# Gathering tokens for a mixture of experts: one transfer of whole 4 KB rows in place of three transfers of 1 KB quarters

## The chip, the cores and the metric

The kernel runs on 1 core of one Trainium2 chip, as one program written for its five engines by hand: TensorE (PE), VectorE (DVE), ScalarE (ACT), GpSimd (POOL) and SyncE (SP). The metric is the device time in microseconds, from the first to the last instruction with what lies around them; the numbers are medians of several runs.

## The reference

Two transformer blocks follow each other over 512 tokens of 1024 floats. The first has a convolution and FFT mixer, a cross attention over 256 memory rows and a mixture of 32 experts, the second two kinds of attention and a dense feed-forward layer. Only the mixture of experts is touched by the change. Cut to what matters:

```python
logits = hf @ w_router + b_router                 # 512 x 32
top_v, top_i = lax.top_k(logits, 4)               # 4 experts of each token
top_w = softmax(top_v)
# for every expert e, over the tokens that chose it:
gu = h[tok] @ w_gate_up[e] + b_gate_up[e]         # 1024 -> 2048
gate = minimum(gu[:, :1024], 7); up = clip(gu[:, 1024:], -7, 7)
glu = gate * sigmoid(1.702 * gate)
y[tok] += top_w * (((up + 1) * glu) @ w_down[e] + b_down[e])
```

All of it is float32. An expert's weights are 8 MB and 4 MB, so 32 experts read 384 MB from HBM. Each expert gets 64 tokens on average.

## The kernel before

A block of the expert stage is one expert with up to `CAP` = 96 slots for tokens (3 groups of 32, `GROUPS` and `QUAD`); a slot without a token is out of bounds for the transfers and is skipped. With these inputs there are 32 blocks. The stage is a loop on each engine.

SP loads the weights in chunks of 1 MB into a ring of 12 slots (`ring_a`, `ring_b`, L557 to L600): 8 chunks of `w_gate_up` and 4 of `w_down` for each block. A load waits on `m_used`, which TensorE raises as it is through with the slot's last chunk.

TensorE (`moe_tensor`, L1940) works on 32 columns of the array at a time: four products side by side, for four quarters j of the output columns. So both operands must have the contraction index on the partitions, and the tokens of a group on 32 free places. `gate_up_open` (L1954) multiplies a one-hot `pick` with the biases and then waits for the tokens, `m_x`. `gate_up_chunk` (L1965, the product is L1970) takes `xe` and a chunk. After the 8 chunks of block n+1 come the 4 `down_chunk` (L1977, product L1984) of block n, with `act_t`. In the midst of the gate and up products `slot_sums` (L1944, product L1947) finds which token sits in which slot; it waits for VectorE's `select`.

The tokens lie in HBM as `h_rows`, 2048 rows of 256 floats: row 4*t+j is quarter j of token t. POOL's `gather` (L743) issues one indirect DMA for each of the three groups (L749). Partition 32*j+s of group g receives quarter j of the token in slot 32*g+s, into `xg[:, g, :]`. The row numbers `idx[0]` are made by `indices` (L1547) on VectorE. VectorE then turns all 32x32 blocks of `xg` with one instruction into `xe` (`x_transpose`, L1575, instruction L1579): in each quarter of the partitions a 32x32 block at a time. The same row numbers, one and two blocks later, serve `scatter` (L752, L757), which adds the weighted outputs onto `x_rows` in HBM.

The order of a block on VectorE is written out at L1613 to L1618: `select` (L1526: which slot holds which token), `indices` (it waits for the scatter two blocks back, since it overwrites its row numbers), `swiglu` (L1581: it takes the sums out of PSUM at L1586 and L1587, waits for ACT's Silu, and makes `act_e` at L1590 and L1593), `pick_row` (L1561), `x_transpose`, and `act_transpose` (L1573: it waits until the down products of the last block are done). `link` puts a semaphore behind an instruction for the next one on VectorE that reads it. Before the loop the first two blocks are done by the same functions, with `route_weights` between them.

`hold` is a small POOL instruction in front of each group of indirect DMAs. `m_gathered` counts 16 for each transfer.

Of the kernel before, what the change touches and what calls it, by code (L numbers as in the profile page):

```python
# [22 lines left out]
GROUPS, QUAD = 3, 32  # L23
CAP = GROUPS * QUAD
PASSES = -(-SEQ // CAP)
MAXB = NE * PASSES
QF = D // 4
# [17 lines left out]
C_EXP = C_TOK + T  # L45
C_OWN = C_EXP + NE
C_QUAD = C_OWN + P
C_EYE = C_QUAD + 1
C_ALL = C_EYE + MAXB + 1

S_CONV, S_GC, S_GF, S_ALL = 0, 12, 16, 20
# [3 lines left out]
def shape_constants():  # L55

    p = np.arange(P)
    c = np.zeros((P, C_ALL), np.float32)
    c[:, C_IDENT:C_IDENT + P] = np.eye(P)
    c[:, C_FLIP:C_FLIP + P] = np.eye(P)[::-1]  # L60
    c[:, C_ONES:C_ONES + P] = 1.0
    c[:, C_STRICT:C_STRICT + P] = p[:, None] < p[None, :]
    c[:, C_NTRI:C_NTRI + P] = -(p[:, None] >= p[None, :]).astype(np.float32)
    c[:, C_NONES:C_NONES + P] = -1.0
    g = np.arange(64)
    w = 2 * np.pi * np.outer(g, g) / 64
    for b in range(2):
        s = slice(64 * b, 64 * b + 64)
        c[s, C_BDC + 64 * b:C_BDC + 64 * b + 64] = np.cos(w) / 8
        c[s, C_BDS + 64 * b:C_BDS + 64 * b + 64] = -np.sin(w) / 8  # L70
    c[:, C_SLOT:C_SLOT + P] = p[None, :]
    n = np.arange(MAXB + 1)
    c[:, C_OWN:C_OWN + P] = np.arange(P)[None, :] % QUAD == p[:, None] % QUAD
    c[:, C_QUAD] = p // QUAD
    c[:, C_TOK:C_TOK + T] = P * np.arange(T)[None, :] + p[:, None] + CAP
    c[:, C_EXP:C_EXP + NE] = np.arange(NE)
    c[:, C_EYE:] = n[None, :] % NE == p[:, None] % NE
    s = np.arange(SEQ)
    w = 2 * np.pi * (np.outer(s, s) % SEQ) / SEQ
    dft = np.stack([np.cos(w), np.sin(w)]).astype(np.float32) * np.float32(SEQ ** -0.5)  # L80
    rel = np.arange(SPAN) - (SEQ - 1)
    dist = np.abs(rel)
    far = np.maximum(dist, 1).astype(np.float32)
    large = 8 + (np.log(far / np.float32(8)) / np.float32(math.log(16)) * np.float32(8)).astype(np.int32)
    bucket = (rel > 0) * 16 + np.where(dist < 8, dist, np.minimum(large, 15))
    onehot = (np.arange(32)[:, None] == bucket[None, :]).astype(np.float32)
    return c, dft.astype(np.float32), onehot
# [26 lines left out]
def program(nc, A, out):  # L114
    ctx = ExitStack()
    with ctx:
# [3 lines left out]
        def at(name, offset, shape, dt=F32):  # L120
            plan[name] = (offset, int(np.prod(shape[1:])) * 4)
            return nc.alloc_sbuf_tensor_at(name, shape, dt, offset=base + offset)

        def sem(n):
            return ctx.enter_context(nc.semaphore(n))
# [24 lines left out]
        K = lambda k: AR + int(k * KB)  # L150
# [12 lines left out]
        probs = at("probs", K(0), [P, 2, T, MEM])  # L163
        probsT = at("probsT", K(48), [P, 2, MT, SEQ])

        xg = at("xg", K(0), [P, GROUPS, QF])
        xe = at("xe", K(4), [P, GROUPS, QF])
        glu = at("glu", K(12), [P, GROUPS, QF])
        up1 = at("up1", K(15), [P, GROUPS, QF])
# [2 lines left out]
        ye = at("ye", K(24), [P, GROUPS, QF])  # L172
        bias_gu = at("bias_gu", K(36), [3 * NE, 2 * D], BF16)
        sel = at("sel", K(40), [P, T, CAP])
        small_i = lambda i: K(41.875) + 32 * i
        slot_s = at("slot_s", small_i(1), [P, 2, GROUPS])
        slot_w = at("slot_w", small_i(9), [P, GROUPS])
        row_f = at("row_f", small_i(10), [P, GROUPS])
        idx = [at(f"idx{i}", small_i(3 + i), [P, GROUPS], I32) for i in range(3)]
# [73 lines left out]
        h_dram = nc.dram_tensor("h_rows", [SEQ * 4, QF], F32, kind="Internal").ap()  # L253
# [4 lines left out]
        cc = lambda c, n=P: const[:, c:c + n]  # L258
# [484 lines left out]
        def gather(pool, n, k):  # L743

            pool.wait_ge(m_idx, n + 1)
            pool.wait_ge(m_x, n)
            hold(pool, k)
            for g in range(GROUPS):
                pool.indirect_dma_start(xg[:, g, :], None, h_dram, bass.IndirectOffsetOnAxis(ap=idx[0][:, g:g + 1].bitcast(U32), axis=0),  # L749
                                        bounds_check=SEQ * 4 - 1, oob_is_err=False).then_inc(m_gathered, 16)  # L750

        def scatter(pool, n, k, rows):  # L752

# [6 lines left out]

        def moe_moves(pool):
            pool.wait_ge(r_table, 1)
            pool.memset(xg[:, :, :], 0.0).then_inc(xg_zero, 1)
            pool.wait_ge(xg_zero, 1)
            pool.wait_ge(m_scat, 16)
            pool.wait_ge(x_set, 16 * T)
            n1 = pool.value_load(n_blk[0:1, 0:1], min_val=NE - 1, max_val=MAXB - 1)
            gather(pool, 0, 0)
            gather(pool, 1, 1)
            with pool.Fori(0, n1) as i:  # L770
                gather(pool, i + 2, i * 2 + 2)
                scatter(pool, i, i * 2 + 3, idx[2])
            scatter(pool, n1, n1 * 2 + 2, idx[1])
# [742 lines left out]
        def moe_vector(dve, link_route):  # L1516
            dve.wait_ge(r_table, 1)
            n1 = dve.value_load(n_blk[0:1, 0:1], min_val=NE - 1, max_val=MAXB - 1)
            steps, base_ = [0], [0]

            def link(i):
                i.then_inc(moe_dve_step, 1)
                steps[0] += 1
                dve.wait_ge(moe_dve_step, base_[0] + steps[0])
# [22 lines left out]
            def indices(n, scattered, gathered, parts=2):  # L1547

                dve.wait_ge(m_pos, n + 1)
                if scattered is not None:  # L1550
                    dve.wait_ge(m_scat, scattered)
                if gathered is not None:
                    dve.wait_ge(m_gathered, gathered)
                dve.tensor_copy(idx[2][:, :], idx[1][:, :])  # L1554
                link(dve.tensor_copy(slot_w[:, :], slot_s[:, 1, :]))
                dve.tensor_copy(idx[1][:, :], idx[0][:, :])
                link(dve.tensor_copy(slot_s[:, 0:parts, :].rearrange("p a g -> p (a g)"), ps[:, 6, 0:parts * GROUPS]))
                link(dve.tensor_scalar(row_f[:, :], slot_s[:, 0, :], 4.0, cc(C_QUAD, 1), ALU.mult, ALU.add))
                dve.tensor_scalar(idx[0][:, :], row_f[:, :], 4.0 * CAP, None, ALU.subtract).then_inc(m_idx, 1)

            def pick_row(n, used):  # L1561

# [5 lines left out]
            flat = lambda b: b[:, :, :].rearrange("p g c -> p (g c)")  # L1568

            def act_transpose(n, used):  # L1570
                dve.wait_ge(m_act, n + 1)
                dve.wait_ge(m_used, used)
                dve.transpose(flat(act_t), flat(act_e)).then_inc(m_at, 1)  # L1573

            def x_transpose(n, used):  # L1575
                dve.wait_ge(m_gathered, n * 48 + 48)
                if used is not None:
                    dve.wait_ge(m_used, used)
                dve.transpose(flat(xe), flat(xg)).then_inc(m_x, 1)  # L1579

            def swiglu(n, used):  # L1581

                dve.wait_ge(m_used, used)
                dve.wait_ge(m_bias_sb, n + 1)
                bias = lambda u: bias_b[:, QF * u:QF * u + QF].unsqueeze(1).to_broadcast([P, GROUPS, QF])
                dve.tensor_tensor(glu[:, :, :], ps[:, 0:GROUPS, 0:QF], bias(0), ALU.add).then_inc(m_sum, 1)  # L1586
                dve.scalar_tensor_tensor(up1[:, :, :], ps[:, 0:GROUPS, QF:2 * QF], 1.0 / ALPHA, bias(1),  # L1587
                                         ALU.mult, ALU.add).then_inc(m_sum, 1)
                dve.wait_ge(m_sum, n * 2 + 2)
                link(dve.tensor_scalar(up1[:, :, :], up1[:, :, :], (1.0 - LIMIT) / ALPHA, (1.0 + LIMIT) / ALPHA, ALU.max, ALU.min))  # L1590
                dve.wait_ge(m_at, n)
                dve.wait_ge(m_glu, n + 1)
                dve.scalar_tensor_tensor(act_e[:, :, :], glu[:, :, :], SILU_TOP, up1[:, :, :], ALU.min, ALU.mult).then_inc(m_act, 1)  # L1593
# [7 lines left out]
            x_transpose(0, None)  # L1601
            route_weights(dve, link_route)
            select(1, 0)
            indices(1, None, 48)
            swiglu(0, 8)
            pick_row(1, 8)
            x_transpose(1, 8)
            act_transpose(0, 8)
            done = steps[0]
            steps[0] = 0  # L1610
            with dve.Fori(0, n1) as i:
                base_[0] = i * 7 + done
                select(i + 2, i + 1)  # L1613
                indices(i + 2, i * 48 + 16, i * 48 + 96)
                swiglu(i + 1, i * 12 + 16)
                pick_row(i + 2, i * 12 + 9)
                x_transpose(i + 2, i * 12 + 16)
                act_transpose(i + 1, i * 12 + 20)  # L1618
            assert steps[0] == 7, steps

        def ffn_vector(dve):
            def gate_up(j):
# [466 lines left out]
```

## Time and profile before

| | us |
|---|---|
| median of 3 runs | 2207.1 (2205.42 to 2207.76) |
| the profiled execution, its own time | 2204.74 |
| its span, first to last instruction | 2202.8 |
| PE busy | 2075.9 (94%) |
| DVE busy | 865.7 (39%) |
| ACT busy | 478.9 (22%) |
| POOL busy | 359.7 (16%) |

The profile describes one execution. The expert stage lies between about 411 and 1462 us of the span, nearly half of it. Its page gives the work of all DMA queues: the hardware queue of SP moved 496.01 MB, the software queue of POOL 24.85 MB, at 237 GB/s over the whole span and 403 to 410 GB/s in most slices of the expert stage. A matmul's time is modelled and pipelined, so a busy TensorE is not one at its peak. In brackets behind a row stands the engine's idle time before the instruction, and who ended it.

### The profile page before, as it was taken

To read this page: it belongs to the slowest core of one execution; us is meant where nothing else is said; L and a number is where in the kernel's file an instruction comes from. 1 tells how busy PE (TensorE), PEld (TensorE's weight loads), DVE (VectorE), ACT (ScalarE), POOL (GpSimd) and SP (SyncE) were. 2 spreads that over 40 slices of the span, in tenths; PEclk is the share of its full clock that TensorE was granted. 3 is DMA by queue.
4 is the path that set the end of the run, shared out by engine and by line. 5 is a ranking of instruction groups with operands and counts; after the bars stand their busy time and mean duration, and the time that the engine had idled before them with its cause. 6 is when DMAs were issued, how large, how long until landed. Compare 5 with 4: busy or idle time off the path is not lost.

```text
span 2202.8 us, 41891 instructions
## 1 busy us (share of the span) xinstructions
PE 2075.9 (94%) x17404; PEld 1255.0 (57%) x17404; DVE 865.7 (39%) x1468; ACT 478.9 (22%) x749; POOL 359.7 (16%) x389
## 2 busy tenths in 40 slices
PE   6999898499999999999999999979998998999998
PEld 5879777234344434433443333337775777888887
DVE  4444434432333233333333333333565433444444
ACT  4242333000000000000000000023445723122221
POOL 1010001112222222222223222231201200000000
PEclk9999999699999999999999999979998999999999
DMA  6325111999999999999999999973111022233230
GB/s 235 116 77 166 58 39 40 354 348 403 405 404 410 405 405 405 410 403 404 403 405 402 404 408 396 399 256 106 58 58 39 1 65 70 76 99 111 77 113 38
DMA packets 157840, 521.53 MB, mean 237 GB/s; under 512 B 16428, under 2 KB 71776, under 8 KB 124928
## 3 DMA queue, kind: packets, MB, share of 16 engines
q1 hardware_dynamic: 137008, 496.01, 57.7%
q0 software_dynamic: 20784, 24.85, 4.7%
q8 instruction: 35, 0.57, 0.1%
q14 instruction: 13, 0.11, 0.0%
HBM read 510.65 MB, written 18.88 MB: 240 GB/s over the span
## 4 chain that ended last, share of the span: by engine, by line
PE 60%; DMA 9%; SPq 4%; DVE 3%; ACT 2%; POOL 1%; issue 1%; ACTq 0%; DVEq 0%; POOLq 0%
PE ps L1970 21%; PE ps L1984 11%; PE ps L390 8%; PE ps L392 8%; PE ps L391 8%; DMA ring_a<-in_w_down 6%; SPq L567 3%; DMA ring_a<-in_w_gate_up 2%; SPq L565 2%; PE ps L1879 1%; PE ps L492 1%; POOL rstd L464 1%; PE ps L1871 1%; PE ps L1889 1%; PE ps L1832 0%
## 5 line engine op out<-in xcount | busy, mean ns | idle before, releaser
L1970 PE MATMUL ps<-ring_a,xe 128*32 128x512 f32 x3912 | 436.0, 596 | 12.2 <-DVE xe L1579 10.6
L1984 PE MATMUL ps<-ring_a,act_t 128*32 128x256 f32 x6000 | 333.5, 379 | 5.5 <-DMA ring_a<-in_w_down 3.8
L1970 PEld LDWEIGHTS ps<-ring_a,xe 128*32 128x32 f32 x3912 | 124.8, 110 | 297.0 <-issue 254.3
L1984 PEld LDWEIGHTS ps<-ring_a,act_t 128*32 128x32 f32 x6000 | 193.6, 110 | 153.0 <-issue 21.5
L1970 PE MATMUL ps<-ring_b,xe 128*32 128x512 f32 x2232 | 251.5, 593 | 0.0
L390 PE MATMUL ps<-xt_hi,hi 128*128 128x512 f32 x576 | 228.8, 397 | 5.6 <-DVE xt_lo L505 4.7
L392 PE MATMUL ps<-xt_hi,lo 128*128 128x512 f32 x576 | 226.4, 393 | 0.0
L391 PE MATMUL ps<-xt_lo,hi 128*128 128x512 f32 x576 | 226.2, 393 | 0.0
L1073 ACT ACTIVATE glu<-glu 128x768 f32<-128x768 f32 x32 | 27.0, 843 | 649.1 <-DVE glu L1586 649.1
L757 POOL DMA_INDIRECT x_rows<-ye,idx x96 | 154.3, 1607 | 37.8 <-issue 37.8
L390 PE MATMUL ps<-hi,xt_hi 128*128 128x512 f32 (+1 forms) x384 | 147.4, 384 | 7.4 <-DVE lo L377 5.2
L1970 PEld LDWEIGHTS ps<-ring_b,xe 128*32 128x32 f32 x2232 | 69.1, 110 | 149.7 <-issue 143.1
L377 DVE TENSOR_TENSOR lo<-raw,hi 128x2048 fp32r<-128x2048 f32 x46 | 106.2, 2314 | 106.1 <-ACT hi L370 103.9
L391 PE MATMUL ps<-lo,xt_hi 128*128 128x512 f32 (+1 forms) x384 | 144.8, 377 | 0.0
L392 PE MATMUL ps<-hi,xt_lo 128*128 128x512 f32 (+1 forms) x384 | 144.8, 377 | 0.0
L1554 DVE COPY idx<-idx 128x3 int32<-128x3 int32 x33 | 5.6, 169 | 338.7 <-DMA x_rows<-ye,idx 332.2
L741 POOL TENSOR_TENSOR held_x<-minus_half 128x1 f32<-128x1 f32 x65 | 12.5, 192 | 713.3 <-ACT ye L1079 368.9
L390 PEld LDWEIGHTS ps<-xt_hi,hi 128*128 128x128 f32 x576 | 109.7, 190 | 29.8 <-DVE xt_lo L505 5.5
L391 PEld LDWEIGHTS ps<-xt_lo,hi 128*128 128x128 f32 x576 | 109.7, 191 | 23.2 <-issue 0.5
L392 PEld LDWEIGHTS ps<-xt_hi,lo 128*128 128x128 f32 x576 | 109.3, 190 | 23.1
L370 ACT ACTIVATE hi<-raw 128x2048 fp32r<-128x2048 f32 x46 | 87.6, 1911 | 103.6 <-PE ps L392 103.6
L749 POOL DMA_INDIRECT xg<-h_rows,idx x99 | 102.7, 1037 | 38.8 <-issue 38.8
(297 smaller groups left out, 2475.4 us busy)
## 6 DMA issues: line engine op xcount, KB each, us to landing
ring_a<-in_w_gate_up SPq DMA_DIRECT2D x163, 1024.0 KB, 20.8
ring_a<-in_w_down SPq DMA_DIRECT2D x125, 1024.0 KB, 23.5
ring_b<-in_w_gate_up SPq DMA_DIRECT2D x93, 1024.0 KB, 19.5
raw<-in_w_in SPq DMA_DIRECT2D x20, 1024.0 KB, 7.7
raw<-in_w_gate SPq DMA_DIRECT2D x11, 1024.0 KB, 5.4
raw<-in_w_up SPq DMA_DIRECT2D x11, 1024.0 KB, 5.4
raw<-in_w_down SPq DMA_DIRECT2D x11, 1024.0 KB, 4.8
raw<-in_w_out SPq DMA_DIRECT2D x8, 1024.0 KB, 5.0
```

The source lines that it names most:

```text
L370: act.activation(hi[:, c % HL, :], raw[:, c % RAW, :], ACT.Copy).then_inc(S.hi_ready, 1)
L377: dve.tensor_tensor(lo[:, c % HL, :], raw[:, c % RAW, :], hi[:, c % HL, :].bitcast(F32), ALU.subtract).then_inc(S.lo_ready, 1)
L390: pe.matmul(dst_, l_hi, r_hi, start=first, stop=False)
L391: pe.matmul(dst_, l_hi, r_lo, start=False, stop=False)
L392: return pe.matmul(dst_, l_lo, r_hi, start=False, stop=last)
L565: sp.dma_start(m_slot(slot), src.squeeze(0) if len(src.shape) == 3 else src).then_inc(m_raw[slot], 16)
L567: sp.dma_start(m_slot(slot).rearrange("p (k n) -> p k n", k=2), src).then_inc(m_raw[slot], 16)
L749: pool.indirect_dma_start(xg[:, g, :], None, h_dram, bass.IndirectOffsetOnAxis(ap=idx[0][:, g:g + 1].bitcast(U32), axis=0), bounds_check=S ...
L757: pool.indirect_dma_start(x_dram, bass.IndirectOffsetOnAxis(ap=rows[:, g:g + 1].bitcast(U32), axis=0), ye[:, g, :], None, bounds_check=SEQ ...
L1073: act.activation(glu[:, :, :], glu[:, :, :], ACT.Silu, scale=ALPHA).then_inc(m_glu, 1)
L1970: last = pe.matmul(ps[QUAD * j:QUAD * j + QUAD, g, :], xe[:, g, QUAD * k:QUAD * k + QUAD], w[:, j, :, :, :], start=k == 0, stop=k == KT - 1)
L1984: last = pe.matmul(y_block(g, j), act_t[:, g, QUAD * (2 * c + h):QUAD * (2 * c + h) + QUAD], w[:, h, QF * j:QF * j + QF], start=c == 0 and ...
```

## The change

The gather becomes one transfer for 96 slots: partition s receives the whole row of 1024 floats of slot s's token. Its row numbers, one for each partition, are made by three more small VectorE instructions: the slot table `slot_s` has, on every partition 32*q+s, the token of slot 32*g+s in column g; the new constant `C_GRP` is one where g equals q, so product and sum pick the token of slot 32*q+s. The table `idx[0]` of the scatter stays as it was.

In `xg` group g now lies in the partitions 32*g to 32*g+31, and quarter q in the columns 256*q to 256*q+255. The transposes therefore read one quarter of the partitions and write another: 12 instructions of 32x256, one for each q and g, in place of one of 128x768. `xe` is the same as before.

`swiglu` is cut in two. `add_bias` (the two additions out of PSUM) stays where it was; the rest comes behind `pick_row` and `x_transpose`.

```diff
-        xg = at("xg", K(0), [P, GROUPS, QF])
+        xg = at("xg", K(0), [P, D])
...
-            for g in range(GROUPS):
-                pool.indirect_dma_start(xg[:, g, :], None, h_dram, bass.IndirectOffsetOnAxis(ap=idx[0][:, g:g + 1].bitcast(U32), axis=0),
-                                        bounds_check=SEQ * 4 - 1, oob_is_err=False).then_inc(m_gathered, 16)
+            pool.indirect_dma_start(xg[0:CAP, :], None, h_dram.rearrange("(s j) c -> s (j c)", j=4),
+                                    bass.IndirectOffsetOnAxis(ap=idx_g[0:CAP, 0:1].bitcast(U32), axis=0),
+                                    bounds_check=SEQ - 1, oob_is_err=False).then_inc(m_gathered, 16)
...
-                dve.tensor_scalar(idx[0][:, :], row_f[:, :], 4.0 * CAP, None, ALU.subtract).then_inc(m_idx, 1)
+                dve.tensor_scalar(idx[0][:, :], row_f[:, :], 4.0 * CAP, None, ALU.subtract)
+                link(dve.tensor_tensor(row_g[:, :], slot_s[:, 0, :], cc(C_GRP, GROUPS), ALU.mult))
+                link(dve.reduce_sum(row_1[:, :], row_g[:, :], AX.X))
+                dve.tensor_scalar(idx_g[:, :], row_1[:, :], float(CAP), None, ALU.subtract).then_inc(m_idx, 1)
...
-                dve.wait_ge(m_gathered, n * 48 + 48)
+                dve.wait_ge(m_gathered, n * 16 + 16)
                 if used is not None:
                     dve.wait_ge(m_used, used)
-                dve.transpose(flat(xe), flat(xg)).then_inc(m_x, 1)
+                for q in range(4):
+                    for g in range(GROUPS):
+                        i = dve.transpose(xe[QUAD * q:QUAD * q + QUAD, g, :], xg[QUAD * g:QUAD * g + QUAD, QF * q:QF * q + QF])
+                i.then_inc(m_x, 1)
...
                 select(i + 2, i + 1)
-                indices(i + 2, i * 48 + 16, i * 48 + 96)
-                swiglu(i + 1, i * 12 + 16)
+                indices(i + 2, i * 48 + 16, i * 16 + 32)
+                add_bias(i + 1, i * 12 + 16)
                 pick_row(i + 2, i * 12 + 9)
                 x_transpose(i + 2, i * 12 + 16)
+                swiglu(i + 1)
                 act_transpose(i + 1, i * 12 + 20)
```

The blocks ahead of the loop are changed in the same way, and the memset of `xg` covers 1024 columns.

## Rows read from the trace of the kernel before

**Rows 1.** Windows: us, each engine's busy time, granted clock, DMA share, GB/s
```profile
500.00:816.30 316.30, 316.30 (x3904) 127.61 (x3900) 104.94 (x250) 25.94 (x60) 82.76 (x80) 1.00 1.03 406
...
1090.80:1449.50 358.70, 353.13 (x4290) 136.80 (x4282) 115.97 (x276) 28.54 (x66) 91.03 (x88) 1.00 1.02 401
```

**Rows 2.** Timeline of VectorE, L1573: start, duration, instruction, idle before
```profile
521.43 0.98 DVE L1573 STREAM_TRANSPOSE act_t<-act_e 128x768 f32<-128x768 f32 x1 [2.85 <-PE ps L1984]
...
1090.83 0.98 DVE L1573 STREAM_TRANSPOSE act_t<-act_e 128x768 f32<-128x768 f32 x1 [3.71 <-PE ps L1984]
...
1449.49 0.98 DVE L1573 STREAM_TRANSPOSE act_t<-act_e 128x768 f32<-128x768 f32 x1 [4.39 <-PE ps L1984]
```

**Rows 3.** Waits of TensorE, 1090 to 1450 us: total, times, longest
```profile
PE ps L1984 <- DMA ring_a<-in_w_down: 3.8, 11, 0.7
```

**Rows 4.** Waits of SP's queue, 1090 to 1450 us
```profile
SPq L567 <- PE ps L1970: 13.9, 5, 3.7
```

**Rows 5.** Windows, around the start of block 1
```profile
458.00:460.00 2.00, 2.00 (x12) 0.45 (x8) 1.97 (x6) 0.00 (x0) 0.00 (x0) 0.50 0.09 31
```

**Rows 6.** DMA queue, 921 to 923 and 920 to 927 us: packets, MB, share
```profile
q0 software_dynamic: 25, 0.10, 12.9%
...
q0 software_dynamic: 144, 0.25, 9.9%
```

**Rows 7.** Windows, a gather and the stretch after it
```profile
920.00:927.00 7.00, 7.00 (x116) 3.55 (x112) 3.53 (x6) 0.84 (x1) 1.49 (x2) 1.00 1.02 411
927.00:933.00 6.00, 6.00 (x112) 3.50 (x108) 1.28 (x2) 0.18 (x1) 0.00 (x0) 1.00 1.02 423
```

**Rows 8.** Timeline of one block, 900 to 933 us
```profile
905.93 0.35 DVE L1545 TENSOR_REDUCE own_q<-own_t 128x6 f32<-128x192 f32 x1
...
908.83 0.39 PE L1947 MATMUL ps<-own_q,const 128*128 128x6 f32 x2
...
916.10 0.17 DVE L1554 COPY idx<-idx 128x3 int32<-128x3 int32 x1 [9.82 <-DMA x_rows<-ye,idx]
...
916.91 0.17 DVE L1559 TENSOR_SCALAR idx<-row_f 128x3 int32<-128x3 f32 x1
...
918.08 1.08 POOL L749 DMA_INDIRECT xg<-h_rows,idx  x1 [0.56 <-issue]
...
920.80 1.00 POOL L749 DMA_INDIRECT xg<-h_rows,idx  x1 [0.31 <-issue]
```

**Rows 9.** Groups by line and form, VectorE: busy us, mean ns, idle before
```profile
L1579 DVE STREAM_TRANSPOSE xe<-xg 128x768 f32<-128x768 f32 x33 | 32.3, 978 | 74.7 <-DMA xg<-h_rows,idx 74.7
...
L1543 DVE STREAM_TRANSPOSE own_t<-own 128x192 f32<-128x192 f32 x32 | 12.1, 378 | 1.1
```

**Rows 10.** Timeline of VectorE, 549 to 554 us
```profile
549.40 0.98 DVE L1579 STREAM_TRANSPOSE xe<-xg 128x768 f32<-128x768 f32 x1 [3.14 <-DMA xg<-h_rows,idx]
553.06 0.98 DVE L1573 STREAM_TRANSPOSE act_t<-act_e 128x768 f32<-128x768 f32 x1 [2.68 <-PE ps L1984]
```

**Rows 11.** Timeline of the first two blocks, 405 to 470 us
```profile
416.83 1.13 POOL L749 DMA_INDIRECT xg<-h_rows,idx  x1 [0.59 <-issue]
...
419.60 1.00 POOL L749 DMA_INDIRECT xg<-h_rows,idx  x1 [0.30 <-issue]
...
426.80 6.74 PE L1970 MATMUL ps<-ring_a,xe 128*32 128x512 f32 x48 [9.97 <-DVE xe L1579]
...
434.98 0.39 PE L1947 MATMUL ps<-own_q,const 128*128 128x6 f32 x2 [1.45 <-DVE own_q L1545]
...
453.56 0.56 DVE L1590 TENSOR_SCALAR up<-up 128x768 f32<-128x768 f32 x1
...
455.03 0.23 DVE L1565 TENSOR_SCALAR pick<-const 96x32 bf16<-96x32 f32 x1
455.17 0.97 DVE L1579 STREAM_TRANSPOSE xe<-xg 128x768 f32<-128x768 f32 x1
...
456.41 4.48 PE L1970 MATMUL ps<-ring_a,xe 128*32 128x512 f32 x24 [0.61 <-DVE xe L1579]
```

More of the change, by code:

```diff
@@ L47 @@
 C_QUAD = C_OWN + P
-C_EYE = C_QUAD + 1
+C_GRP = C_QUAD + 1
+C_EYE = C_GRP + GROUPS
 C_ALL = C_EYE + MAXB + 1
@@ L74, in shape_constants @@
     c[:, C_QUAD] = p // QUAD
+    c[:, C_GRP:C_GRP + GROUPS] = p[:, None] // QUAD == np.arange(GROUPS)[None, :]
     c[:, C_TOK:C_TOK + T] = P * np.arange(T)[None, :] + p[:, None] + CAP
@@ L164, in program @@
         probsT = at("probsT", K(48), [P, 2, MT, SEQ])
-        xg = at("xg", K(0), [P, GROUPS, QF])
+        small_i = lambda i: K(41.875) + 32 * i
+        xg = at("xg", K(0), [P, D])
+        idx_g = at("idx_g", small_i(2), [P, 1], I32)
+        row_g = at("row_g", small_i(11), [P, GROUPS])
+        row_1 = at("row_1", small_i(12), [P, 1])
         xe = at("xe", K(4), [P, GROUPS, QF])
@@ L174, in program @@
         sel = at("sel", K(40), [P, T, CAP])
-        small_i = lambda i: K(41.875) + 32 * i
         slot_s = at("slot_s", small_i(1), [P, 2, GROUPS])
@@ L762, in moe_moves @@
             pool.wait_ge(r_table, 1)
-            pool.memset(xg[:, :, :], 0.0).then_inc(xg_zero, 1)
+            pool.memset(xg[:, :], 0.0).then_inc(xg_zero, 1)
             pool.wait_ge(xg_zero, 1)
@@ L1575, in x_transpose, with add_bias @@
             def x_transpose(n, used):
-                dve.wait_ge(m_gathered, n * 48 + 48)
+                dve.wait_ge(m_gathered, n * 16 + 16)
                 if used is not None:
                     dve.wait_ge(m_used, used)
-                dve.transpose(flat(xe), flat(xg)).then_inc(m_x, 1)
-            def swiglu(n, used):
+                for q in range(4):
+                    for g in range(GROUPS):
+                        i = dve.transpose(xe[QUAD * q:QUAD * q + QUAD, g, :], xg[QUAD * g:QUAD * g + QUAD, QF * q:QF * q + QF])
+                i.then_inc(m_x, 1)
+            def add_bias(n, used):
                 dve.wait_ge(m_used, used)
@@ L1588, in swiglu @@
                                          ALU.mult, ALU.add).then_inc(m_sum, 1)
+            def swiglu(n):
                 dve.wait_ge(m_sum, n * 2 + 2)
@@ L1603, in moe_vector @@
             select(1, 0)
-            indices(1, None, 48)
-            swiglu(0, 8)
+            indices(1, None, 16)
+            add_bias(0, 8)
             pick_row(1, 8)
             x_transpose(1, 8)
+            swiglu(0)
             act_transpose(0, 8)
@@ L1611, in moe_vector @@
             with dve.Fori(0, n1) as i:
-                base_[0] = i * 7 + done
+                base_[0] = i * 9 + done
                 select(i + 2, i + 1)
-                indices(i + 2, i * 48 + 16, i * 48 + 96)
-                swiglu(i + 1, i * 12 + 16)
+                indices(i + 2, i * 48 + 16, i * 16 + 32)
+                add_bias(i + 1, i * 12 + 16)
                 pick_row(i + 2, i * 12 + 9)
                 x_transpose(i + 2, i * 12 + 16)
+                swiglu(i + 1)
                 act_transpose(i + 1, i * 12 + 20)
-            assert steps[0] == 7, steps
+            assert steps[0] == 9, steps
         def ffn_vector(dve):
```

## The prediction

> **What bounds the kernel now.** I read the expert stage's windows first [rows 1]: from 500 to 1450 us TensorE is busy all the time at first and nearly all of it later (316.30 of 316.30 us, 353.13 of 358.70) and the 16 DMA engines are too (share 1.02 to 1.03). Two resources are full at once, so the question is which ends last. The timeline of one instruction per block, the transpose of `act_e` (L1573), gives the period [rows 2]. From 521.43 to 1090.83 us there are 18 blocks: 31.63 us each, the same to 0.01. From 1090.83 to 1449.49 us there are 11: 32.61 us each. The first period is TensorE's own. The second is not: in it TensorE waits for weight chunks [rows 3], and SP hardly waits any more for TensorE to free a slot (13.9 us, 5 times, in 360 us [rows 4]): the loads are behind. So DMA needs about 32.6 us per block all along. The ring of 12 slots is full when the stage begins (at 458 to 460 us the DMA share is 0.09, for want of free slots [rows 5]), loses 32.61 - 31.63 = 0.97 us of lead per block, and is drained after 20 blocks. The total is then start of the stage plus DMA work of all 31 blocks behind it. This has two consequences. Whatever adds DMA time to a block counts 31 times, not 11. Whatever makes TensorE late by under 0.97 us in a block costs nothing once the lead is shrinking; but a delay of the start counts in full, because DMA stands still then for want of free slots.
>
> **DMA work of the gather.** The aim of one 4 KB row would be fewer, larger pieces. Between 921 and 923 us the software queue's 25 packets carry 0.10 MB, 4 KB each, and in the whole gather 144 packets carry 0.25 MB [rows 6]: rows of 1 KB already leave four to a packet. Bytes are the same after. How much the present form costs beyond its bytes: in the 7 us of a gather the engines move 411 GB/s, in the 6 us after it 423 [rows 7]; 7 x (1 - 411/423) = 0.20 us per block is the most that could vanish. The scatter, which moves its rows in another way, is left alone by the change.
>
> The other side: a transfer's semaphore counts 16, one for each engine, so 96 slots are 6 rows per engine, and a row is now whole where before its four quarters were four descriptors on different partitions. Used rows stand at the front: 0.25 MB is 62 rows of 4 KB. If an engine takes six neighbouring rows, some ten engines move 24 KB and five nearly nothing, against 16 KB on average: 8 KB more at 406/16 = 25.4 GB/s is 0.32 us for the fullest engine, and a weight chunk lands only with its last engine. Part of it replaces the unevenness that the third transfer has now (it holds the few tokens beyond 64). No row shows how 96 rows are dealt out, so the bounds are -0.20 and +0.32 us per block, and +0.65 if all used rows fall on eight engines (16 KB more). I take +0.10: a third of the way to the middle case, since that one is nearest to how the slots are numbered. 31 x 0.10 = +3.1 us; ends -6.2 and +10, in the extreme +20.
>
> The Trainium skill, "DMA: Bandwidth & Descriptors", section "The descriptor swizzle", speaks against the change: it gives a formula by which a 128-partition transfer puts partitions 0 to 63 on engines 0 to 7 and the rest on 8 to 15. It states this for 128 partitions only. If 96 went the same way, the used rows would sit on half of the engines, which is the +0.65 above; whether it holds no row here shows.
>
> **VectorE's turn.** One transpose of 128x768 (978 ns) becomes twelve of 32x256. Rows: 128x192 takes 378 ns, 128x768 978 ns [rows 9], so 1.04 ns per column and 178 ns fixed; 256 columns are 444 ns. An instruction with no wait before it starts a little before the last one ends: pick lasts 0.23 us, and the transpose behind it starts 0.14 after it [rows 11], 0.09 of overlap. 12 x (0.444 - 0.09) + 0.09 = 4.3 us; with a few gaps I take 4.4, +3.4 against now. Bounds: columns alone, 12 x 0.267 = 3.2 us; no overlap, 5.3 us. The Trainium skill says the same of small tiles ("VectorE: DVE Perf Modes", section "The TRN2 errata — SBUF-src ops pay a fixed extra latency per instruction"): the fixed part is paid per instruction, and it advises 512 elements or more. Its formula 58 + FD cycles at 0.96 GHz would make an estimate of 327 ns each, 3.9 us in all; the two rows decide for 4.4.
>
> In a running block this is beside other work. xe must be ready when the down products end; that is where L1573 starts. The landing of the gather, where L1579 starts after its wait, leads L1573 by 3.66 us in the tightest block (549.40 to 553.06 [rows 10]). After the change POOL issues one transfer, 2.72 us before today's third (918.08, 920.80 [rows 8]), with three small VectorE operations (row_g, row_1, idx_g) ahead of it, each like L1559, 0.17 us [rows 8], +0.5; and all bytes behind the one issue, +1.2 us (0.25 MB at half of 411 GB/s). So it lands about 1 us earlier: 4.7 us of room in the tightest block against 4.4. At 5.3 us the tightest would be 0.6 late, under the 0.97 that DMA forgives. The moved rest of `swiglu` (L1590 and L1593, 1.47 us, 453.56 to 455.03 [rows 11]) is behind the transposes now; act_e can be late by some 1.4 us, then `select` too. It ends at 906.28 (905.93 + 0.35) and TensorE takes own_q at 908.83 [rows 8], 2.5 us of room. `indices` waits for the scatter to land anyway (9.82 us idle [rows 8]). So a price of 0 in the loop; `add_bias` keeps its place, and ACT's Silu (after the first sum) is earlier than its reader by more than before. The memset of the wider xg and one DMA issue instead of three on POOL are hidden: POOL waits longer than it works.
>
> **The start is not covered.** [rows 11] Block 0: TensorE's first product at 426.80 waits for xe. m_idx comes +0.5 late; the one issue replaces the third of 419.60 by the first of 416.83, -2.77; bytes behind it +1.2; transposes +3.4. Sum +2.3 us (bounds 0, with short transposes and a landing at once, and +4.8 with nothing landing earlier and long ones). `route_weights` and `select` stand behind it on VectorE and TensorE waits for them at 434.98, so the shift stays. Block 1: xe now starts at 455.17, after all of swiglu; after the change pick starts at 453.56, where L1590 does, xe 0.14 later, and ends at 453.70 + 4.4 = 458.1 against 456.14: +2.0 us (bounds +0.8, +2.9), and TensorE waits for it as it does now (456.41). DMA idles behind both (the second one: [rows 5]), so both go straight into the end. TensorE's clock is already at 0.50 of full speed (1.2 of 2.4 GHz) at 458 to 460 after its idle time [rows 5]; more idle may lengthen that, at most by a microsecond. Together +4.3 (0.8 to 7.7).
>
> **Sum.** +4.3 + 3.1 = +7.4 us. The profiled execution took 2204.7 us (2202.8 and 1.9 around the span): 2212.1. It lay 2.4 us below the median of the runs, 2207.1, so I say 2214.5 for the median.
>
> **Rivals.**
> 1. Faster: the gather's framing is the DMA's loss and vanishes. For it: DMA is full and everything counts 31 times. Against: packets of 4 KB already, and at most 0.20 us to win. -6.2 + 4.3 = -1.9, 2205 us; it falls below 2203, the point from which this is a gain that can be told, only if the start costs under 2 us, or if a block saves 0.3 us. At 0.97 saved DMA no longer binds, and the most is -10.7 (11 blocks x 0.97) + 4.3 = 2201 us. Chance 0.18, of it 0.12 below 2202.7.
> 2. DMA work unchanged, only the start: 2207.1 + 4.3 = 2211 us. For it: same bytes, same packets; against: the front-loaded slots. Chance 0.27.
> 3. Used rows on half of the engines: 31 x 0.65 = +20, 2231 us. It decides from 0.5 us per block. Chance 0.10.
> 4. VectorE late in every block: at 978 ns per transpose (the duration of the full one) they take 11 us, xe is 6 us late in the tightest block and, I estimate, 4 in a usual one; TensorE stalls 31 times, +124, 2331 us. Decides when twelve take over 6 us. Chance 0.02.
> Forecast (start and mild unevenness, 2212 to 2219): chance 0.43.
>
> This kernel can be told from itself at about 0.2%, 4.4 us. Below 2202.7 lie 0.12 of rival 1. Between 2202.7 and 2211.5 lie its other 0.06 and rival 2: 0.33. Above: 0.43 + 0.10 + 0.02 = 0.55. The range is 2204 to 2228: it leaves out the gain and half of rival 3.
>
> **What would show it.** L1573's period: 31.63 us at first, and over 32.6 in the late stretch, with the first waits for weight chunks before 1090 us; shorter late periods refute the unevenness. The twelve transposes: 4.4 us from first to last. TensorE's first product of xe 2.3 us later, that of block 1 4.3 us later. POOL: 33 issues of the gather instead of 99. With a period of 31.63 us to the end with the start as said, rival 1 would be right and my DMA term wrong.

## The result, and the profile after

Median 2243.9 us (2239.6 to 2245.2, 4 runs) against 2206.3 us of the kernel before on the same chip (2205.1 to 2207.8, 4 runs): a ratio of 1.0169, 95% interval 1.0152 to 1.0185. That is 37.7 us slower, where +7.4 us was forecast and 2228 us was the upper end of the range. The profiled execution has a span of 2241.7 us.

Three groups of the page of the kernel after (busy us, mean ns | idle before, releaser). VectorE is busy for 1023.2 us in place of 865.7, but still only 46% of the span. What matters are TensorE's two idle times, 36.0 and 15.5 us, against 12.2 and 5.5 at the same two operations before.

```profile
L1986 PE MATMUL ps<-ring_a,xe 128*32 128x512 f32 x3912 | 440.0, 600 | 36.0 <-DVE xe L1589 34.5
L2000 PE MATMUL ps<-ring_a,act_t 128*32 128x256 f32 x6000 | 333.4, 381 | 15.5 <-DMA ring_a<-in_w_down 13.0
...
L1589 DVE STREAM_TRANSPOSE xe<-xg 32x256 f32<-32x256 f32 x396 | 172.2, 435 | 117.7 <-DMA xg<-h_rows,idx_g 112.6
```

The windows of [rows 1], after. The DMA share is 1.03 and 1.02 as before, but the engines move 393 and 390 GB/s, not 406 and 401. A share that stays full while the rate falls means that each byte takes an engine longer.

```profile
500.00:816.30 316.30, 306.64 (x3672) 120.84 (x3668) 141.02 (x365) 23.36 (x54) 62.48 (x59) 0.99 1.03 393
1090.80:1449.50 358.70, 342.50 (x4181) 133.90 (x4174) 159.27 (x411) 26.80 (x61) 64.37 (x63) 1.00 1.02 390
```

The start, after, in the timeline, to be laid beside [rows 11].

```profile
417.09 1.08 POOL L753 DMA_INDIRECT xg<-h_rows,idx_g  x1 [0.63 <-POOL held_x L746]
426.05 5.37 DVE L1589 STREAM_TRANSPOSE xe<-xg 32x256 f32<-32x256 f32 x12 [9.72 <-DMA xg<-h_rows,idx_g]
...
431.48 7.73 PE L1986 MATMUL ps<-ring_a,xe 128*32 128x512 f32 x48 [14.43 <-DVE xe L1589]
...
458.33 0.23 DVE L1573 TENSOR_SCALAR pick<-const 96x32 bf16<-96x32 f32 x1
458.47 5.36 DVE L1589 STREAM_TRANSPOSE xe<-xg 32x256 f32<-32x256 f32 x12
...
464.07 4.23 PE L1986 MATMUL ps<-ring_a,xe 128*32 128x512 f32 x24 [4.97 <-DVE xe L1589]
```

TensorE's first product is 4.7 us later (431.48 for 426.80), that of block 1 7.7 us later (464.07 for 456.41).

L1573 of [rows 2] is L1581 now. Here are an early and a late stretch of it.

```profile
465.45 0.98 DVE L1581 STREAM_TRANSPOSE act_t<-act_e 128x768 f32<-128x768 f32 x1
...
532.97 0.98 DVE L1581 STREAM_TRANSPOSE act_t<-act_e 128x768 f32<-128x768 f32 x1
...
1319.09 0.98 DVE L1581 STREAM_TRANSPOSE act_t<-act_e 128x768 f32<-128x768 f32 x1
...
1353.17 0.98 DVE L1581 STREAM_TRANSPOSE act_t<-act_e 128x768 f32<-128x768 f32 x1
...
1387.27 0.98 DVE L1581 STREAM_TRANSPOSE act_t<-act_e 128x768 f32<-128x768 f32 x1
```

Two blocks from 465.45 to 532.97 take 67.5 us, 4.3 more than twice 31.63. Late ones take 34.1, where before they took 32.6. And no idle time stands behind any of these lines (5 of the 32 in the stage have some): in [rows 2] VectorE waited 2.9 to 4.4 us for the products here, now it mostly comes late itself. TensorE's waits, 456 to 1500 us (us in total, times, longest), give both causes: xe, of which the kernel before had only the 0.61 us of [rows 11] here, and weight chunks [rows 3].

```profile
PE ps L1986 <- DVE xe L1589: 20.1, 14, 5.0
PE ps L2000 <- DMA ring_a<-in_w_down: 13.0, 9, 1.7
```

So there were two suspects. **R**: the whole rows make the DMA side dearer. **V**: the twelve transposes make xe late. The runs below take the change apart. Each was timed beside the kernel before, whose medians lay between 2205.0 and 2206.3 us. Ratios are to these; all other differences are between medians, and between runs that were not timed together the baseline's 1.3 us has to be allowed for.

### The profile page after: what moved, and what is told of

Same layout as the page of the kernel before. It is cut to its first block, busy times and chain, and to the rows that moved or that the text cites. A ratio compares the mean times of both kernels' runs of the same rounds, so it can differ in the third digit from the quotient of the medians.

```text
span 2241.7 us, 42283 instructions
## 1 busy us (share of the span) xinstructions
PE 2082.8 (93%) x17404; PEld 1254.9 (56%) x17404; DVE 1023.2 (46%) x1930; ACT 479.2 (21%) x749; POOL 293.0 (13%) x323
## 4 chain that ended last, share of the span: by engine, by line
PE 47%; DMA 14%; SPq 6%; DVE 6%; issue 3%; ACT 2%; POOL 2%; POOLq 0%; ACTq 0%; DVEq 0%
PE ps L1986 13%; PE ps L395 8%; PE ps L397 7%; PE ps L396 7%; PE ps L2000 7%; DMA ring_a<-in_w_down 5%; DMA x_rows<-ye,idx 5%; DMA xg<-h_rows,idx_g 4%; SPq L572 3%; SPq L570 3%; DVE xe L1589 2%; PE ps L1895 1%; POOL x_rows L762 1%; POOL rstd L469 1%; PE ps L1887 1%
## 5 line engine op out<-in xcount | busy, mean ns | idle before, releaser
L2000 PE MATMUL ps<-ring_a,act_t 128*32 128x256 f32 x6000 | 333.4, 381 | 15.5 <-DMA ring_a<-in_w_down 13.0
L1589 DVE STREAM_TRANSPOSE xe<-xg 32x256 f32<-32x256 f32 x396 | 172.2, 435 | 117.7 <-DMA xg<-h_rows,idx_g 112.6
```

The costliest lines, as they stand in the source:

```text
L1589: i = dve.transpose(xe[QUAD * q:QUAD * q + QUAD, g, :], xg[QUAD * g:QUAD * g + QUAD, QF * q:QF * q + QF])
L2000: last = pe.matmul(y_block(g, j), act_t[:, g, QUAD * (2 * c + h):QUAD * (2 * c + h) + QUAD], w[:, h, QF * j:QF * j + QF], start=c == 0 and ...
```

## Taking the change apart

**e1, the order and the cut alone.** The kernel before, with `add_bias`, `pick_row`, `x_transpose`, `swiglu` in the new order, and

```
-                dve.transpose(flat(xe), flat(xg)).then_inc(m_x, 1)
+                for q in range(4):
+                    for g in range(GROUPS):
+                        i = dve.transpose(xe[QUAD * q:QUAD * q + QUAD, g, :], xg[QUAD * q:QUAD * q + QUAD, g, :])
+                i.then_inc(m_x, 1)
```

> The kernel before (three transfers of 1 KB quarters) with the new order on VectorE and its transpose cut into twelve of 32x256 that stay in their partition quarter. Theory A (VectorE's twelve transposes are the loss: they take 5.37 us, start to start 0.448, and nothing else covers them): most of the +37 us is here, 2228 to 2245, with TensorE waiting for xe in many blocks and the same 0.448 us from start to start. Rival B (the gather of whole rows makes every block's DMA work longer, and that is the loss): only the start's shifts, +4 to +8 us, 2210 to 2215, late periods of L1573's transpose still 32.6 us.

Measured: 2209.3 us, ratio 1.0019 (1.0010 to 1.0029). The cut alone is no explanation of 37.7 us.

**e2, the whole rows with the new order, without the twelve.** The changed kernel with one transpose of 128x768 again (`dve.transpose(flat(xe), xg[:, 0:GROUPS * QF])`). The work is the same, but the tokens reach the products in wrong places.

> The changed kernel (one transfer of whole rows, new order) with one transpose of 128x768 in place of the twelve, so that the tokens reach the products in wrong places. Theory A: the loss goes with the transposes, 2200 to 2210. Rival B: the late periods stay near 33.5 us and the time at 2225 to 2240. If both sides add, e1 and e2 each give a part and their parts sum to 37 us.

Measured: 2231.7 us, 1.0110 (1.0093 to 1.0127): +26.2 us on the kernel before's 2205.5, with the transpose as fast as before. The period is 31.63 us up to 805.30 and longer from there, 285 us sooner than in [rows 2].

```profile
805.30 0.98 DVE L1581 STREAM_TRANSPOSE act_t<-act_e 128x768 f32<-128x768 f32 x1 [1.70 <-PE ps L1997]
838.73 0.98 DVE L1581 STREAM_TRANSPOSE act_t<-act_e 128x768 f32<-128x768 f32 x1 [2.68 <-PE ps L1997]
...
1444.05 0.98 DVE L1581 STREAM_TRANSPOSE act_t<-act_e 128x768 f32<-128x768 f32 x1 [3.73 <-PE ps L1997]
```

From 838.73 to 1444.05 are 18 blocks of 33.63 us. Before it was 32.61: DMA needs 1.02 us more per block.

**e4, the order alone** (the kernel before, only the order of the calls edited).

> The kernel before with the new order on VectorE alone (add_bias, pick, x_transpose, then the rest of swiglu). xe of block 1 is ready 1.5 us earlier at the start, in the loop nothing waits for it. Theory: -1 to -2 us, 2204 to 2206. Rival: act_e later makes select late and with it own_q: no gain or +1 to 3 us.

Measured: 2202.2 us, 0.9982 (0.9972 to 0.9991): the order is worth 3 to 4 us by itself, and e1 stands 7 us above it. This is the price of a cut into twelve whose pieces stay in their quarter.

## The DMA side: two causes that add

The tokens of an expert are numbered from slot 0 (`C_SLOT`), and 41 to 92 of 96 slots are used, counted by the gather's 4 KB packets in each block. Two things could cost: which engine gets which rows, and what the dealing does to other transfers. One edit gives six neighbouring slots tokens of different rank (e5), one makes the transfer 128 rows, the last 32 out of bounds (e6), and e7 has 128 rows and a numbering that gives each engine four of the first 64.

```
 e5  +    c[:, C_SLOT:C_SLOT + CAP] = 16 * (s % 6) + s // 6
 e6  -            pool.indirect_dma_start(xg[0:CAP, :], None, ...  idx_g[0:CAP, 0:1]
     +            pool.indirect_dma_start(xg[:, :], None, ...      idx_g[:, 0:1]
 e7  e6, and
     +    run, at = s % QUAD // 4, s % 4
     +    c[:, C_SLOT:C_SLOT + CAP] = np.select([s < QUAD, s < 2 * QUAD], [16 * at + run, 64 + 8 * at + run], 16 * at + 8 + run)
```

All three stand on e2, with one transpose, and so leave the tokens in wrong places as e2 does.

> e2 (whole rows, one transpose, tokens in wrong places in the products) with the 96 slots numbered so that neighbouring six hold one, two, three ... of each sixteen tokens: if engine k takes rows 6k to 6k+5, every engine gets 4 of 64. Theory C (the loss of e2 is the fullest engine): late periods back from 33.6 to 32.3 us or less, 2200 to 2212. Rival E (4 KB packets take 208 ns instead of 164 and slow the weights' because they write where other engines write): the packets stay at 200 ns or over, and most of the loss stays, 2220 to 2232.

Measured: 2208.9 us, 1.0013 (1.0004 to 1.0023), 23 us below e2: which ranks share an engine is one cause. Its late period is 32.7 us (from 1025 us on), where e2 had 33.6. Rival E's sign came too: the gather's 4 KB packets still take 205 ns, 208 in e2. So E is right on the packets and wrong on the loss.

> e2 with 128 row numbers in place of 96, the last 32 out of bounds. If 128 partitions are dealt out in runs of four with 0 to 63 on engines 0 to 7, used rows sit on eight engines, 8 each, but each engine writes its own partitions as for the weights. Theory C: worse than e2, 2240 or more. Rival E: packets back at 164 ns, and better than e2, under 2225.

Measured: 2214.8 us, 1.0044 (1.0027 to 1.0061), 17 us below e2, though the used rows now sit on few engines as well.

> e6 with the slots numbered so that under that dealing each engine gets 4 of 64 rows. Theories C and E both want this: packets of 164 ns, late periods near 32.1 us, 2193 to 2204. If neither is right it stays with e2 at 2225 to 2235.

Measured: 2193.4 us, 0.9947 (0.9930 to 0.9963), 38 us below e2: about the sum, and more than the 29.5 us that the whole rows cost (e4 to e2), because the kernel before has some unevenness itself (e3, below). The four kernels make a square. The numbering takes off 22.8 us with 96 rows (e2 to e5) and 21.3 with 128 (e6 to e7); the 128 rows take off 17.0 with ranks in order (e2 to e6) and 15.4 with spread ones (e5 to e7). The period of 31.63 us holds to the end of the stage, so TensorE bounds it throughout, and the time could show no more gain on the DMA side. e7 has everything of the change but the twelve transposes, the three index operations too, and it is as fast as e8 below (2194.4), which has three transfers of quarters with spread slots. So one transfer of whole rows, dealt well, neither costs nor wins anything that these two can show.

```profile
1401.26 0.98 DVE L1583 STREAM_TRANSPOSE act_t<-act_e 128x768 f32<-128x768 f32 x1 [2.47 <-PE ps L1999]
1432.89 0.98 DVE L1583 STREAM_TRANSPOSE act_t<-act_e 128x768 f32<-128x768 f32 x1 [3.71 <-PE ps L1999]
```

What both edits mend is seen in the DMA view, 500 to 1430 us (queue: packets, MB, share of 16 engines' time). First the kernel before:

```profile
q1 hardware_dynamic: 64102, 360.83, 95.1%
q0 software_dynamic: 16901, 15.22, 7.6%
```

Then e2:

```profile
q1 hardware_dynamic: 62438, 350.76, 94.6%
q0 software_dynamic: 15410, 14.64, 7.8%
```

Then e6:

```profile
q1 hardware_dynamic: 63459, 357.69, 94.4%
q0 software_dynamic: 16466, 14.88, 7.4%
```

And q1 alone of e5, then of e7:

```profile
q1 hardware_dynamic: 63418, 357.39, 94.9%
```

```profile
q1 hardware_dynamic: 65350, 364.69, 95.4%
```

Share times 16 x 930 us over MB is engine time per MB. For q1, the weights, it is 39.2 us before, 40.1 in e2, 39.5 in e5, 39.3 in e6 and 38.9 in e7. Nothing about the weights was changed; their transfers are slower beside the 96-row gather, most of all with ranks in order. A block loads 12 chunks, 12.6 MB, so 0.9 x 12.6 / 16 = 0.7 us per block of e2's 1.02. The single packets say the same: a 4 KB packet of the gather takes 208 ns on average in e2, 205 in e5, 165 before, 162 in e6 and 160 in e7, and an 8 KB packet of weights 327, 319, 316, 317 and 312 ns.

The number of rows decides the gather's own packets (208 and 205 ns with 96, 162 and 160 with 128), the numbering hardly. The weights' packets answer to both. But the means do not hold the whole price of the numbering: e6 has almost the engine time of the kernel before, 39.3 us per MB, and is still 9 us slower than it; and it is slower than e5, which has 39.5. What is left there is, as we read it, that a chunk waits for the fullest engine; no record shows this wait. How the rows are dealt was not read from a record that names an engine; that the numbering derived from it brings what it should is the evidence. The Trainium skill, "DMA: Bandwidth & Descriptors", states both halves: "The descriptor swizzle", the formula by which each engine of a 128-partition transfer writes its own port of the memory, from which e7's numbering is derived; and "Why a DMA increments its semaphore by 16 and not by 1", that 96 partitions are split over 16 engines as well. If an engine takes six neighbouring partitions, as e5 bears out, they do not fit the formula's groups of four, and engines write at each other's ports. That this is what lengthens the packets is an inference, which e6's return to 162 ns and e5's 205 agree with.

**e3, the same unevenness in the kernel before.** Its three transfers have 128 rows each; only `C_SLOT` is edited, so that neighbouring ranks go round the eight groups of four partitions.

```
+    c[:, C_SLOT:C_SLOT + CAP] = 8 * (4 * (s // QUAD) + s % 4) + s % QUAD // 4
```

> The kernel before with another numbering of the slots: the tokens of an expert go round the eight runs of four partitions in each quarter, where before the few beyond 64 all stood in the first run. Bytes, instructions and packets' total are the same. Theory C (a block's DMA time is that of the fullest engine, gather and scatter together): late periods fall from 32.6 towards 32.2 us and the time by 4 to 11 us, 2195 to 2202. Rival D (DMA is bound by the sum over all engines): no change, 2204 to 2208.

Measured: 2196.5 us, 0.9956 (0.9939 to 0.9972). So the numbering cost the kernel before 9 us, and the period stays at 31.63 us to 1312.69.

**e8, e3 with the new order.**

> Both gains without the change's gather: three transfers of quarters and one transpose as before, slots spread as in e3, VectorE's order as in e4. If they add, -9 - 3 = -12 us, 2193 to 2195; if e4's gain was the start's, it must add, since TensorE's period is the bound in e3.

Measured: 2194.4 us, 0.9944 (0.9928 to 0.9961). Of the kernels that do the whole work it is the fastest, and the one to keep. Of the order's 3 to 4 us some 2 are left, less than what two medians of this kernel can tell apart.

## VectorE's side: why twelve cost 7 us in one kernel and 24 in another

**e11 and e9, both mendings in the complete changed kernel.** e11 has e5's numbering, e9 the 128 rows and the numbering of e7; both keep the twelve transposes.

> The changed kernel, complete, with one edit: C_SLOT numbers the tokens as in e5, so that six neighbouring rows (one DMA engine's by the dealing of 96 rows) hold tokens of different rank. With one large transpose the edit took 23 us off (2231.7 to 2208.9). Theory A (unevenness is the cause on the DMA side, VectorE's side adds): 2244 - 23 = 2221 us (2214 to 2228), late blocks of about 32.7 us. Rival E (lateness of xe hides what DMA gives back): 2232 us or more, with waits for xe of over 30 us. If unevenness were not what the edit mends: 2240 us or more.

Measured: 2221.1 us, 1.0068 (1.0051 to 1.0085), 12 us above e5, as the changed kernel is 12 above e2.

> The changed kernel, complete, with two edits: the gather names 128 rows (the last 32 out of bounds, not brought) and C_SLOT numbers the tokens so that each DMA engine gets four of the first 64 (by the dealing that e7 bore out). With one large transpose these two edits took the whole-row gather from 2231.7 to 2193.5 us. Theory A (the DMA side and VectorE's side add, and VectorE's side costs its start only): 2193.5 plus what twelve transposes cost in the start, about 7 us: 2200 us (2196 to 2204), blocks of 31.6 us nearly to the end, TensorE's waits for xe still seen but small. Theory B (twelve transposes hurt more where DMA is not the bound, since then no lateness is forgiven): TensorE's period rises above 31.63 in about half of the blocks, by 2 us or more each: 2215 us or more. Rival C (the twelve transposes disturb the DMA side too, by the port to the memory): w_down waits of over 10 us come back: 2210 us with blocks of 32.5.

Measured: 2217.3 us, 1.0055 (1.0038 to 1.0072): 24 us above e7. A and C are wrong; no w_down wait is left among the six largest. The time is B's, and TensorE waits for xe in 15 blocks, 4.8 us in block 1 and up to 1.9 in the others; its period alternates in most of the stage:

```profile
883.39 0.98 DVE L1583 STREAM_TRANSPOSE act_t<-act_e 128x768 f32<-128x768 f32 x1
...
917.08 0.98 DVE L1583 STREAM_TRANSPOSE act_t<-act_e 128x768 f32<-128x768 f32 x1
...
947.81 0.98 DVE L1583 STREAM_TRANSPOSE act_t<-act_e 128x768 f32<-128x768 f32 x1
```

33.7, then 30.7 us. The chain of waits from 900 to 1000 us, by line, first the kernel before, then e9, tells what ends last:

```profile
by line: PE ps L1970 66.5%; PE ps L1984 32.2%; PE ps L1947 1.0%; PE ps L1959 0.9%
```

```profile
by line: PE ps L1988 41.7%; PE ps L2002 20.8%; DMA xg<-h_rows,idx_g 15.9%; DMA x_rows<-ye,idx 10.4%; issue 5.8%; DVE xe L1591 4.5%; POOL x_rows L764 1.9%; ACT ye L1086 0.7%; PE ps L1965 0.6%; POOL held_x L748 0.6%; DVE row_f L1565 0.5%; DVE
```

Before, TensorE follows on TensorE. In e9 the path leaves it: the scatter of a block, then the indices, the gather, the twelve transposes, and only then TensorE again. That chain is a little longer than the time TensorE leaves it, so each microsecond more in it is paid in about every second block. VectorE made it longer twice: the transposes take 5.37 us (4.4 forecast, 0.98 before), and the three operations behind `idx` delay the issue by some 0.5.

e1's twelve fit the forecast, though. The view by tile, one block each: e1, then the changed kernel (ns: shortest, median, longest).

```profile
L1581 DVE STREAM_TRANSPOSE xe<-xg x12: 390/396/442, 905.5 to 909.5; 32x256 f32<-32x256 f32 x12
```

```profile
L1589 DVE STREAM_TRANSPOSE xe<-xg x12: 432/436/440, 919.4 to 924.3; 32x256 f32<-32x256 f32 x12
```

The first to the last start is 4.0 us in e1 and 4.9 in the changed kernel. e12 and e13 ask whether the quarters do it.

**e12, e9 with nothing crossing** (`xg[QUAD * q:QUAD * q + QUAD, QF * g:QF * g + QF]` is read).

> As e9 (2217.3 us, TensorE period alternating between 30.8 and 33.7 us), but each of the twelve transposes reads its own quarter of partitions, so that nothing crosses (tokens land misplaced, the work is the same). Theory F: crossing is what makes them 5.37 us in place of 4.40 (e1, whose twelve stayed in their quarter), and xe ends a chain of scatter, indices, gather and transposes that is longer than TensorE's block by little; so each us taken from that chain comes back in about every second block. Expect 4.4 us from first to last and 2207 us (2202 to 2212). Theory A (the extra loss of e9 is not VectorE's chain): 2214 us or more. If the crossing is free and the 5.37 us come from the whole-row tile: 5.37 us and 2217 us again.

Measured: 2202.4 us, 0.9984 (0.9974 to 0.9993), and 4.40 us for the twelve:

```profile
933.42 4.41 DVE L1591 STREAM_TRANSPOSE xe<-xg 32x256 f32<-32x256 f32 x12 [2.06 <-DMA xg<-h_rows,idx_g]
```

Theory F holds: 0.97 us per block less in this chain is worth 14.9 us.

**e13, e9 with the loops over q and g exchanged.**

> As e9, complete, but the twelve transposes go by input quarter (g outside, q inside), so the quarter read stays for four and the quarter written changes each time; in the changed kernel it is the other way round, and instructions start 0.448 us apart. In e1, where the quarter changed, the next began 0.404 us after the last, and elsewhere 0.326 to 0.369. Theory G (a change of the quarter read costs the overlap): about 4.5 us from first to last and 2208 us. Theory H (any transpose that writes another quarter than it reads loses it): 5.37 us and 2217 us, as e9. Theory I (a change of the quarter written costs more): over 5.4 us.

Measured: 2217.2 us, 1.0045 (1.0031 to 1.0059), no gain:

```profile
940.18 5.37 DVE L1591 STREAM_TRANSPOSE xe<-xg 32x256 f32<-32x256 f32 x12 [1.73 <-DMA xg<-h_rows,idx_g]
```

G is wrong. H's number came, but its reason is not shown: no run crosses while both quarters stay the same, and H does not give the 0.40 us of e1 below. In e13 the quarter read stays for four instructions and the quarter written changes; in e9 it is the other way round; both lose the overlap each time. In e1 both stay for three, and the first instruction of a quarter starts 0.40 us after the one before it, the other two after 0.37 and 0.33, where in e9 all are 0.45 apart. In the trace an instruction that changes a quarter starts 0.01 us after the end of the one before it, the others 0.06 to 0.07 us ahead of that end. The Trainium skill has this as a rule ("VectorE: DVE Perf Modes", section "Two Vector instructions with no wait between them"): an instruction that reads or writes another quarter than the one before it is held until that one has finished. All three runs agree with it. It was not weighed in the prediction, and it speaks against this change: each of the twelve has its own pair of quarters, so no order helps.

**e14, e8 with the twelve of e1**: DMA is not the bound, nothing crosses, three transfers.

> e8 (the kernel before with the spread slots and the new order, 2194.4 us, three transfers a block) with the one transpose cut into twelve of 32x256, each in its own quarter (4.4 us from first to last, as in e1). Theory A (twelve transposes cost their +7 us of e4 to e1 wherever they stand): 2201 us (2198 to 2204). Theory B (where DMA no longer binds, no lateness is forgiven, so the cost rises): 2207 us or more, with TensorE's periods above 31.63 in most of the blocks. By theory F the chain is 1.5 us shorter than that of e9 in VectorE's part and up to 0.7 longer in the landing: between the two, 2201 to 2209.

Measured: 2201.0 us, 0.9981 (0.9971 to 0.9990), 6.6 us above e8, as in e1 over e4. So where the chain has room, it costs nothing that DMA no longer forgives lateness: TensorE's waits for xe, 456 to 1500 us, are only 1.0 us outside block 1.

```profile
PE ps L1979 <- DVE xe L1582: 5.0, 4, 4.0
```

Where the chain has none, it does seem to count: the same twelve crossing transposes cost 12 us where DMA binds in the late stage (e2 to the changed kernel, e5 to e11) and 24 where TensorE does (e7 to e9). That the difference is DMA's forgiveness fits the prediction's own rule for a shrinking lead; no run tests it by itself.

**e10, the changed kernel with all of swiglu ahead again.**

> The changed kernel with the whole of swiglu ahead of pick_row and x_transpose again, as before the change. Before the change the new order alone was worth 4 us of 2206 (e4). Theory A (VectorE's lateness for xe is part of the loss): the twelve transposes start 1.5 us later in each block, so TensorE waits for xe in more blocks and longer than the 20 us now: 2250 us or more (2248 to 2265). Rival D (the moved rest of swiglu, which now makes act_e late, is what costs): 2236 us or less, with the waits for xe no longer than now. No change (2240 to 2247): the order has nothing to do with it.

Measured: 2242.5 us, 1.0166 (1.0149 to 1.0183), no difference from the changed kernel. Neither A nor D: block 1 starts 2.05 us later (466.12 for 464.07), but the waits for xe are 17.2 us, 10 times, in place of 20.1, 14 times. What the new order wins at the start it loses again in the loop; the runs do not show where in the loop.

## Why the prediction was wrong, by its steps

- **What bounds the kernel** was right: DMA binds through the ring, costs on it count in all blocks (e2: +1.02 us per block in the late stage became 29.5 us above e4, which has the same order), and the period leaves 31.63 us sooner.
- **DMA work, +0.10 us per block: this step failed.** Measured +1.02, outside the bounds of -0.20 to +0.65. The unevenness was named with its mechanism, six neighbouring rows to an engine, and taken at a third of its middle case of +0.32; but e5 takes 23 us off e2, 0.7 us per block. That the gather's dealing makes the *weights'* packets slower (39.2 to 40.1 us per MB, some 0.7 us per block by itself, of which e5 takes back two thirds) was no term of the sum at all. Bytes, packet size and the fullest engine were weighed, but not what the gather does to another queue's packets. Rival 3, half of the engines, +20 us, was the nearest in size and wrong in its picture: used rows on too few engines are what e6 has, and it is faster than e2.
- **"It lands about 1 us earlier": failed.** The sum counted from the third issue and took 1.5 us (2.72 less 1.2) off the time between first issue and data, then gave 0.5 back for the index operations. The kernel before, whose first issue is at 416.83 [rows 11]:

```profile
425.76 0.98 DVE L1579 STREAM_TRANSPOSE xe<-xg 128x768 f32<-128x768 f32 x1 [9.66 <-DMA xg<-h_rows,idx]
```

  From the first issue to the transposes are 8.9 us there and 9.0 us now (417.09 to 426.05); in the loop the medians, 500 to 1430 us, are 8.75 and 8.8. So two issues fewer brought the data no earlier. The numbering gives back some of the 1.5 us (8.1 in e5, 8.0 in e7); why the rest does not come is open.
- **Twelve transposes, 4.4 us:** the size is right where nothing crosses (4.40) and just over its upper bound with the crossing (5.37; bound 5.3). The overlap of 0.09 us was read from `pick` and the transpose behind it, which both start in the first quarter.
- **Price 0 in the loop: failed**, by the two steps above. Room in the tightest block of [rows 10] was 3.66 us. Taking 4.4 us of transposes and 0.5 of indices from it without the earlier landing leaves xe 1.2 us late; in the loop TensorE waited up to 2.50 us for it, 15 us in 13 blocks. And a late xe costs more than its wait:

```profile
531.49 4.48 PE L1986 MATMUL ps<-ring_a,xe 128*32 128x512 f32 x24 [2.50 <-DVE xe L1589]
```

  These 24 products take 4.48 us; 24 others take 2.78. The windows show why: TensorE is busy all the time behind the stall, but the granted clock averages 0.63 and 0.62, so part of the stretch is at the lower of its levels of 1.2 and 2.4 GHz.

```profile
529.00:531.30 2.30, 0.00 (x0) 0.00 (x0) 2.20 (x7) 1.74 (x5) 0.42 (x2) 1.00 1.03 411
531.50:533.00 1.50, 1.50 (x12) 0.54 (x16) 1.34 (x3) 0.00 (x0) 1.20 (x2) 0.63 1.03 410
533.00:536.00 3.00, 3.00 (x24) 0.77 (x20) 2.97 (x10) 0.00 (x0) 2.69 (x2) 0.62 1.02 397
536.00:540.00 4.00, 4.00 (x40) 1.22 (x36) 2.32 (x4) 0.00 (x0) 0.37 (x1) 1.00 1.12 306
```

- **The start, +4.3 us: mis-sized.** Measured +7.7, the upper end of its bounds (0.8 to 7.7). Block 0: the transposes began 0.3 us later than before, not 1.1 earlier, and the transposes took 4.4 more, not 3.4: +4.7 in place of +2.3. Block 1: 1.0 us more of transposes, +3.0 in place of +2.0.

In the sum: the whole rows with the new order +26.2 (e2), the twelve transposes +12.2 on top of it (e2 to the changed kernel); 0.7 too much against 37.7, within what the baselines differ. Of the twelve, about 7 are the cut and the start where three transfers are used (e4 to e1, e8 to e14), and 9 in e12 over e7. That the rest is the crossing is argued from e9 and e12, where it is worth 14.9; in the changed kernel itself it was not run alone.

## What to carry to other kernels

Before one indirect transfer replaces several, ask how its rows are dealt to the DMA engines, how many of them each engine really moves, and what it does to the packets of other queues: here 128 rows with 32 out of bounds beat 96 rows by 15 to 17 us, and a numbering of the slots was worth 21 to 23, and 9 in the kernel before. When work is added on an engine that looks idle, follow the chain that goes round through scatter, indices and gather, and measure its slack from data landed to data needed: an engine at 39% can hold the shortest slack in the kernel. Cutting a VectorE operation into quarters costs at each piece (4.40 us for twelve in place of 0.98 for one), and 0.08 us more for each when no two consecutive pieces stay in the same quarters.

## What had not been expected of the hardware

- Transfers of one queue slow down those of another without more bytes: weights' 8 KB packets take 327 ns beside the 96-row gather, 319 beside it with spread slots, 317 beside the 128-row one and 312 beside that with spread slots.
- The last data packet of the 96-row gather ends 7.1 to 8.3 us after its issue (changed kernel, 500 to 1430 us, median 7.8) and does not follow the number of rows: 7.7 us with 41 and with 92. In e7 it does: 5.6 us with 41, 6.6 with 70, 7.6 with 92.
- Twelve transposes of 32x256: 4.40 us when the quarters stay for three instructions, 5.37 us when at least one of them changes each time, whether mostly the one read (e9) or the one written (e13).
- A TensorE stall of 2.50 us was followed by 4.5 us at a granted clock of 0.62 to 0.63, with the DMA share at 1.02 to 1.03.
